# Decode read-out in column groups, output projection taken by token halves, 16 dropped columns, and two state stores ahead of two loads

## The reference, cut to what matters

```python
z, xbc, dt = jnp.split(u @ w_in, ...)
xs, Bm, Cm = jnp.split(silu(conv(xbc)), ...)
y, final = ssd_chunked(xs, dt, A, Bm, Cm, ssm_state, chunk)   # C @ start state, decayed, plus the part within a chunk
y = (y + d_skip * xs) * silu(z)
yg = y.reshape(b, L, SSM_GROUPS, D_INNER // SSM_GROUPS)
y = yg * rsqrt(mean(yg * yg) + EPS) * norm_w
return y @ w_out, new_conv, final
```

## Time and profile before

| | us |
|---|---|
| median of 3 runs | 1124.11 |
| the profiled execution | 1121.49 |
| its span, first to last instruction | 1119.7 |
| PE busy | 1037.6 (93%) |
| DVE busy | 609.9 (54%) |
| ACT busy | 452.2 (40%) |
| POOL busy | 369.3 (33%) |
| mean granted clock of PE | 0.965 |

### The profile page before, as it was taken

How to read it: one execution, slowest core, us unless ns; L and a number is a source line. 1 busy time by engine, 2 the same in 40 slices (tenths; PEclk the granted TensorE clock), 3 DMA queues, 4 the chain that set the end, 5 groups by cost and what they waited for, 6 DMA issues and landing times.

```text
span 1119.7 us, 18856 instructions
## 1 busy us (share of the span) xinstructions
PE 1037.6 (93%) x7568; PEld 962.5 (86%) x7568; DVE 609.9 (54%) x1438; ACT 452.2 (40%) x780; POOL 369.3 (33%) x274
## 2 busy tenths in 40 slices
PE   5999999999999899978888999899989999898978
PEld 4998899889997899768878988898889988898858
DVE  4125421544135322547794679747796567965772
ACT  5334622362334522563224355144542435434252
POOL 1431134213311333116340445315362164540530
PEclk9999999999999999989998899998999999997979
DMA  6422123322223222011325533154331552407202
GB/s 181 154 81 95 39 76 102 111 81 90 79 60 117 89 76 82 20 38 38 98 79 135 151 98 123 40 154 142 88 123 40 153 157 73 150 13 207 76 12 81
DMA packets 144119, 106.37 MB, mean 95 GB/s; under 512 B 10258, under 2 KB 135364, under 8 KB 143840
## 3 DMA queue, kind: packets, MB, share of 16 engines
q1 hardware_dynamic: 117160, 92.10, 26.8%
q10 hardware_dynamic: 26872, 13.06, 4.5%
HBM read 92.42 MB, written 16.79 MB: 98 GB/s over the span
## 4 chain that ended last, share of the span: by engine, by line
PE 65%; DVE 16%; issue 5%; DMA 4%; ACT 3%; POOL 3%; SPq 1%; ACTq 0%; DVEq 0%; POOLq 0%
PE pp L1010 16%; PE pp L1012 15%; PE pp L1011 15%; DVE cv L1658 4%; DVE y_lo L1807 2%; PE pT_ L1248 2%; DMA w_raw_buf<-in_w_attn_out 2%; POOL w_lo_buf L547 2%; PE pS L1106 1%; PE pO L1081 1%; PE pT_ L1298 1%; POOL seg L585 1%; DVE cv L1656 1%; DMA seg<-a_scratch 1%; DVE z L1799 1%
## 5 line engine op out<-in xcount | busy, mean ns | idle before, releaser
L547 POOL TENSOR_TENSOR w_lo_buf<-w_raw_buf,w_hi_buf 128x512 fp32r<-128x512 f32 x226 | 309.6, 1401 | 589.5 <-ACT w_hi_buf L611 453.4
L1010 PE MATMUL pp<-h_hi,w_hi_buf 128*128 128x280 f32 x1280 | 394.7, 308 | 8.4 <-DVE rb L1632 3.2
L1011 PE MATMUL pp<-h_lo,w_hi_buf 128*128 128x280 f32 x1280 | 376.6, 294 | 0.0
L1012 PE MATMUL pp<-h_hi,w_lo_buf 128*128 128x280 f32 x1280 | 376.6, 294 | 0.0
L1010 PEld LDWEIGHTS pp<-h_hi,w_hi_buf 128*128 128x128 f32 x1280 | 245.7, 192 | 20.6 <-issue 12.0
L1011 PEld LDWEIGHTS pp<-h_lo,w_hi_buf 128*128 128x128 f32 x1280 | 245.8, 192 | 4.9 <-issue 4.3
L1012 PEld LDWEIGHTS pp<-h_hi,w_lo_buf 128*128 128x128 f32 x1280 | 245.4, 192 | 0.0
L611 ACT ACTIVATE w_hi_buf<-w_raw_buf 128x2048 fp32r<-128x2048 f32 (+1 forms) x57 | 107.8, 1892 | 31.2 <-PE pp L1012 11.0
L1471 DVE TENSOR_TENSOR x<-x,pp 128x280 f32<-128x280 f32 x128 | 56.3, 444 | 99.6 <-PE pp L1012 99.2
L1010 PE MATMUL pp<-y_hi,w_hi_buf 128*128 128x280 f32 x256 | 80.3, 314 | 13.3 <-DVE y_lo L1807 8.7
L1010 PE MATMUL pp<-og_hi,w_hi_buf 128*128 128x280 f32 x256 | 76.3, 298 | 5.1 <-DVE og_lo L1577 4.6
(11 more groups left out here) (286 smaller groups left out, 1688.5 us busy)
## 6 DMA issues: line engine op xcount, KB each, us to landing
w_raw_buf<-in_w_attn_in SPq DMA_DIRECT2D x16, 1024.0 KB, 5.1
w_raw_buf<-in_w_ssm_in SPq DMA_DIRECT2D x16, 1024.0 KB, 5.5
w_raw_buf<-in_w_attn_out SPq DMA_DIRECT2D x8, 1024.0 KB, 6.5
s_in<-in_state_ssm SPq DMA_DIRECT2D x32, 256.0 KB, 4.2
out<-s_in SPq DMA_DIRECT2D x32, 256.0 KB, 3.5
seg<-a_scratch ACTq DMA_DIRECT2D x16, 512.0 KB, 4.1
w_raw_buf<-in_w_ssm_out SPq DMA_DIRECT2D x8, 1024.0 KB, 5.5
w_raw_buf<-in_w_attn_in SPq DMA_DIRECT2D x8, 512.0 KB, 6.5
```

The lines of the kernel that those rows point to most:

```text
L547: ins = pool.tensor_tensor(w_lo_buf[n % LO_SLOTS][:, piece], raw[n % RAW_SLOTS][:, piece], w_hi_buf[n % HI_SLOTS][:, piece].bitcast(F32), ...
L1010: pe.matmul(dst, hi[:, k, cols], a_hi[:, k, tk], start=(k == 0), stop=False)
L1011: pe.matmul(dst, hi[:, k, cols], a_lo[:, k, tk], start=False, stop=False)
L1012: mm = pe.matmul(dst, lo[:, k, cols], a_hi[:, k, tk], start=False, stop=(k == depth - 1))
```

## The change

- `y_of` is replaced. `y_quad` takes four sequences: for each, 32 columns of weights (`c_own`, the sequence's 4 columns of C among zeros, made by ACT) stand in a column group of their own, and the transposed state streams with 512 columns. Two quads accumulate in one bank. ACT copies the bank out, and `turn_y` multiplies it back into the old layout with four products. There are four `sT` buffers where there were two.
- z and the mixer's output projection leave out the 16 meta columns: halves of 272.
- The output projection goes by blocks of tiles: all first halves, then all second halves (blocks of 4 tiles; in the last stage one block of 8). DVE adds in that order, puts the low parts of y's second part behind the first two adds, and one tap behind each later one.
- DVE's `add_skip(g, 0)` stands behind `prepare(g, 1)` and one evacuation of z.
- SP issues two state stores, then two loads.

```diff
+def out_order(stage):
+    blocks = (range(0, 8),) if stage == STAGES - 1 else (range(0, 4), range(4, 8))
+    return [(t, half) for tiles in blocks for half in range(2) for t in tiles]
+def span(kind, stage, half):
+    if kind == "z" or kind == "out" and stage >= GROUPS:
+        n = SEQ // 2 + SAMPLE // 2
+        return slice(N_META + half * n, N_META + (half + 1) * n)
+    return slice(half * HALF, (half + 1) * HALF)
...
         def part_of(part):
-            return slice(EARLY, T) if part else slice(0, EARLY)
+            return slice(EARLY, T) if part else slice(N_META, EARLY)
...
                     sp.dma_start(rows(ssm_sample, b), s_in[u % STATE_SLOTS][:, :, :]).then_inc(sn_out[u % STATE_SLOTS], 16)
-                    if b + STATE_SLOTS < DEC_B:
-                        load_state(b + STATE_SLOTS)
+                    if b + 1 == DEC_B - STATE_SLOTS:
+                        for later in range(STATE_SLOTS, DEC_B):
+                            load_state(later)
...
+                if i == 1:
+                    act.wait_ge(c_zero, 1)
+                    act.wait_ge(act_ready, k + 1)
+                    step, last_b = SAMPLE + DEC_S, (DEC_B - 1) * DEC_S
+                    act.activation(c_own[:, 0:(DEC_B - 1) * step].rearrange("p (b s) -> p b s", s=step)[:, :, 0:DEC_S],
+                                   bc[:, 1, PROMPT:PROMPT + last_b].rearrange("p (b s) -> p b s", s=DEC_S), ACT.Copy)
+                    act.activation(c_own[:, (DEC_B - 1) * step:], bc[:, 1, PROMPT + last_b:T],
+                                   ACT.Copy).then_inc(c_own_ready, 1)
...
-                    act.activation(sT[b % 2][:, :], pO[:, b % 2, :], ACT.Copy).then_inc(sT_ready, 1)
+                    act.activation(sT[b % 4][:, :], pO[:, b % 2, :], ACT.Copy).then_inc(sT_ready, 1)
                 split_hi()
+                act.wait_ge(yo_done, 3 * g + 2)
+                act.activation(sT[1][:, :], pT_[:, 1, :], ACT.Copy).then_inc(yo_copied, 1)
...
-                def y_of(b):
-                    pe.wait_ge(sT_ready, DEC_B * g + b + 1)
-                    c0 = PROMPT + b * DEC_S
-                    for t in range(HEADS):
-                        mm = pe.matmul(pT_[:, 1, t * SAMPLE + b * DEC_S:t * SAMPLE + (b + 1) * DEC_S],
-                                       sT[b % 2][:, t * P:(t + 1) * P], bc[:, 1, c0:c0 + DEC_S], start=True, stop=True)
+                def y_quad(i):
+                    pe.wait_ge(c_own_ready, g + 1)
+                    for j in range(4):
+                        b = 4 * i + j
+                        pe.wait_ge(sT_ready, DEC_B * g + b + 1)
+                        mm = pe.matmul(pT_[SAMPLE * j:SAMPLE * (j + 1), 1, :], c_own[:, b * SAMPLE:(b + 1) * SAMPLE],
+                                       sT[j][:, :], start=(i == 0), stop=(i == 1))
                     mm.then_inc(yo_done, 1)
...
-                    y_of(2 * pair)
-                    y_of(2 * pair + 1)
+                    if pair % 2:
+                        y_quad(pair // 2)
+            def turn_y(g):
+                pe.wait_ge(yo_copied, g + 1)
+                for t in range(HEADS):
+                    mm = pe.matmul(pT_[:, 1, t * SAMPLE:(t + 1) * SAMPLE], sT[1][:, t * P:(t + 1) * P],
+                                   cst[:, C_SUM4:C_SUM4 + SAMPLE], start=True, stop=True)
...
-                    for t in range(8):
-                        tile_of("out", s - 1, t)
+                    for t, half in out_order(s - 1):
+                        project("out", s - 1, t, half)
...
                 project("z", s, *part.pop(0))
+                turn_y(g)
...
-                    low_y(g - 1, 1)
...
-                    for t in range(8):
-                        add_out(s - 1, t)
-                        for n in (2 * t, 2 * t + 1):
-                            if n < 12:
-                                conv_tap(g, 3 + n // 4, n % 4)
+                    for n, (t, half) in enumerate(out_order(s - 1)):
+                        add_out(s - 1, t, (half,))
+                        if n < 2:
+                            low_y(g - 1, 1, (2 * n, 2 * n + 1))
+                        elif n < 14:
+                            conv_tap(g, 3 + (n - 2) // 4, (n - 2) % 4)
...
-                add_skip(g, 0)
                 prepare(g, 1)
                 evac_z()
+                add_skip(g, 0)
```

More of the change, by code:

```diff
@@ L90, in shape_constants, with add @@
     return c
+def out_order(stage):
[6 more added lines that the diff above has]
+    return slice(half * HALF, (half + 1) * HALF)
 def plan():
     slabs, halves = [], []
-    def add(kind, stage, count, tiles_per_slab, first=0):
-        for i in range(first, first + count):
+    def add(kind, stage, count, tiles_per_slab):
+        for i in range(count):
             slabs.append((kind, stage, i))
+            if kind == "out" and stage >= GROUPS:
+                continue
             for t in range(tiles_per_slab * i, tiles_per_slab * (i + 1)):
@@ L102, in add @@
                     halves.append((kind, stage, t, half))
+        if kind == "out" and stage >= GROUPS:
+            halves.extend((kind, stage, t, half) for t, half in out_order(stage))
     for s in range(GROUPS):
@@ L534, in _ @@
             pool.memset(eps[:, 1:2], EPS * P).then_inc(ones_ready, 1)
+            pool.memset(c_own[:, :], 0.0).then_inc(c_zero, 1)
             done = [0]
@@ L993, in project @@
                 cols = slice((tile % per) * P, (tile % per + 1) * P)
-                tk = slice(half * HALF, (half + 1) * HALF)
+                tk = span(kind, s, half)
                 if kind == "out":
@@ L1429, in result @@
                 pe.transpose(dst[0:32, 512:640], x[:, t, PROMPT:T], ident).then_inc(yt_done, 1)
-            for t in range(8):
-                tile_of("out", STAGES - 1, t)
-                if t:
+            for n, (t, half) in enumerate(out_order(STAGES - 1)):
+                project("out", STAGES - 1, t, half)
+                if n == 0:
+                    final_state(GROUPS - 1)
+                if half and t:
                     result(t - 1)
-                else:
-                    final_state(GROUPS - 1)
             result(7)
@@ L1456, in bank @@
             def bank(kind, s, tile, half):
-                j = half_no[(kind, s, tile, half)]
+                j, tk = half_no[(kind, s, tile, half)], span(kind, s, half)
                 dve.wait_ge(p_done, j + 1)
-                return pp[:, j % 2, 0:HALF]
+                return pp[:, j % 2, 0:tk.stop - tk.start]
             def scaled(dst, kind, s, tile, parts=(0, 1)):
@@ L1466, in scaled, with add_out @@
                                       ALU.mult).then_inc(p_evac, 1)
-            def add_out(s, tile):
-                for half in range(2):
-                    tk = slice(half * HALF, (half + 1) * HALF)
+            def add_out(s, tile, halves=(0, 1)):
+                for half in halves:
+                    tk = span("out", s, half)
                     dve.tensor_tensor(x[:, tile, tk], x[:, tile, tk], bank("out", s, tile, half),
@@ L1800, in norm_y, with low_y @@
                                              ALU.mult, ALU.mult).then_inc(yn_ready, 1)
-            def low_y(g, part):
+            def low_y(g, part, tiles=range(HEADS)):
                 tk, done = part_of(part), 8 * g + 4 * part
-                for t in range(HEADS):
+                for t in tiles:
                     dve.wait_ge(og_hi, 4 * GROUPS + done + t + 1)
@@ L1938, in _ @@
                 low_y(GROUPS - 1, part)
-            for t in range(8):
-                add_out(STAGES - 1, t)
+            for t, half in out_order(STAGES - 1):
+                add_out(STAGES - 1, t, (half,))
 _INS = ["x_prompt", "x_sample", "cache_k", "cache_v", "state_conv", "state_ssm", "meta_tokens", "norm_w",
```

28 lines of the change are left out of this document (17 added, 11 removed).

## The result

| | before | after |
|---|---|---|
| median (range, runs) | 1124.27 us (1123.35 to 1124.81, 4) | 1084.67 us (1084.22 to 1087.12, 4) |
| profiled execution, span | 1121.49, 1119.7 | 1085.0, 1083.2 |
| mean granted clock | 0.965 | 0.98 |

The ratio of the times is 0.9656, 95% interval 0.964 to 0.9671: about 38.7 us less, where 42.5 were forecast for the profiled execution, which lost 36.5.

The account below looks back on a forecast made before the run. PE was taken as the bound (busy 93%, 65% of the chain of waits). Terms of 17.2 + 3.2 + 10.5 + 6.6 + 5.0 = 42.5 us off a 1124.1 us median gave 1082 us, range 1068 to 1102.

Parts of the forecast that it names:

- Term 1: Output projections of stages 1 to 3: the new order shortens each window to 26.0 us, 17.2 us less in all.
- term 3: State read-out, groups 0 to 2: two quads and `turn_y` replace four blocks, 10.5 us less.
- term 4: Behind the read-out, groups 0 to 2: two thirds of the half-clock loss of 9.9 us goes, 6.6 us less.
- term 5: Group 3: last state load issued some 2.5 us earlier, four read-out blocks replaced by quads; 5.0 us less.
- Waits for `x` adds and none for low parts: Sign in the output projections, expected with windows at about 26 us: PE waits for DVE's additions only.
- Term 2: z and the last output projection: eight columns fewer save 3.3 ns a matmul, 3.2 us less.
- No wait for a state load in group 3: Sign in group 3: PE, which stood 1.43 us for the last sequence's load, no longer waits.
- Clock as before: Rival: the clock falls as before, since transposes and small products stay; 1088 us, chance 0.15.
- DVE takes the gain: Rival at the output stage: DVE's slots stand in PE's way, windows of 29 us; 1091 us, chance 0.14.
- No overlap of four: Rival in the read-out: column groups run one after another, 3.4 us a quad, 20 more; 1102 us, chance 0.12.
- Slower: Rival in the read-out: quads run one after another and at half clock; 1133 us, chance 0.03.

Follow-up runs that it names:

- e2: Kernel after, with the mixer's output projection tile by tile again and DVE's low parts ahead of the additions: 1100.02 us.
- e7: Kernel after, keeping PE's new output order, but DVE makes all low parts of y's second part before the additions: 1095.47 us.
- e1: Kernel after, with z and the output projection in halves of 280 columns again: 1089.37 us.
- e3: Kernel after, with the old read-out of the states (`y_of` and its additions) put back: 1099.62 us.
- e4: Kernel after, with all eight read-out products of a group one after another in one column group: 1094.91 us.
- e8: Kernel after, POOL's subtraction and ACT's clamp for one head of eight, exponent scaled, part of the computation left out: 1069.61 us.
- e6: Kernel after, with ACT issuing the next segment load ahead of this segment's decays: 1083.44 us.
- e9: Kernel after, with the four `ec` loads issued behind the read-out's copy and not between two state copies: 1090.49 us.
- e11: Kernel after, with POOL's subtraction for the full segments moved to ACT as a bias, one activation per head, nothing left out: 1083.17 us.

## Why the prediction was right, point by point

The time of 1084.67 us lies 2.7 us above the forecast of 1082. For the profiled execution, from which the terms were read, it was 1079, and that one took 1085.0: 6 us off. Term 1 held in mechanism and size. Of the others the mechanisms held in the main but not the sizes: term 3 brought far less than was put down, term 4 more, and term 5 came out for another reason than the one given. That the sum came out as near as it did is in part luck.

**Term 1, the output projection: right.** 25.93 us a window for a forecast of 26.0, so 17.5 us for 17.2. Undoing the order (e2) costs 13.3 in the whole. What the prediction named as late next, DVE, is what remains: PE is idle 0.4 us of 25.5. "Waits for `x` adds and none for low parts" was half right: 1.3 us for additions, and 1.5 for low parts, 0.9 of them in the third window. That the interleaving matters as much as the order (e7) is what the step-by-step play of DVE's queue had assumed.

**Term 2, columns: somewhat too large.** A matmul is 2.4 ns shorter and not 3.3, so 960 of them give 2.3 us for 3.2; e1, with 1536, gives 2.2 to 4.7 us. The columns of the output windows, put in term 1, bring nothing there.

**Term 3, the read-out: right where it stands, too large in the sum.** The quad was put at 0.96 us and takes 1.00; the second one 1.31 for 1.26; `turn_y` 0.80 for 0.95. Four column groups run side by side. In the Trainium skill ("TensorE: Matmul & The Clock Gate", Part 3) three column tiles give 2.38 times and four row tiles 3.07. Here four column tiles of 32 columns take 1.06 us against 3.62 in one group: 3.4 times. The step that failed is the missing one. Nothing was said of the rounds behind the read-out, where the segment's chain of 8.0 us a round came out as the bound once PE arrived early. e3, e4 and e8 show it: 22 us of terms 3 to 5 undone cost 12.4, 20 us of serial passes cost 8.2, and the chain cut short gives 15.0. By the stages, groups 0 to 2 lost 14.9 us outside the output windows. Their three half-clock stretches are some 10.2 of that by estimate, and the columns 1.4, so about 3 us are left of the 10.5 of this term.

**Term 4, the clock: right and rather more.** Two thirds of 9.9 us were taken; the stretches are gone in all three groups, 20.4 us at half clock and so some 10.2 us for 6.6. They are gone from the three boundaries as well, where the stall for low parts had been. e3 brings back those behind the read-out, e7 those at the boundaries (6.8, 3.4 and 3.4 us). e2 has the waits for low parts again and only one of the three (3.4 us at 831.8), so what made them is not shown. The rule weighed against it, that transposes don't keep the clock (the Trainium skill, same page, Part 4), did not make the drops stay. The transposes are as they were, and quads of 512 columns stand in place of the long blocks of 4. No run takes the transposes away, and none sets the blocks' going apart from the quads' coming.

**Term 5, group 3: wrong in its cause.** "No wait for a state load in group 3" failed. Both loads are issued right behind the two stores, in one piece:

```profile
983.74 0.94 SPq L528 DMA_DIRECT2D out<-s_in  x2
986.11 1.34 SPq L503 DMA_DIRECT2D s_in<-in_state_ssm  x2
```

PE can start on the first only at 991.5, 5.4 us after its issue. The DMA engines are busy 97% of the time from 986 to 993; the transfers of `seg` and `ec` (five by ACT from 985.69 to 988.8) are under way at the same time. PE has run ahead meanwhile, so it waits longer than before:

```profile
991.54 0.66 PE L1303 MATMUL pO<-cst,s_in 128*128 128x128 f32 x4 [2.61 <-DMA s_in<-in_state_ssm]
993.37 1.12 PE L1303 MATMUL pO<-cst,s_in 128*128 128x128 f32 x4 [1.17 <-DMA s_in<-in_state_ssm]
```

Behind it the clock falls for 10.2 us, for 13.7 in the earlier trace rows. From the output projection at the head of its stage to the end the kernel is 11.7 us shorter (138.0 for 149.7), of which 5.0 are the window's and 6.7 are left, for 5.0 of this term and 1.3 of term 2. The load didn't bring them. By estimate most came with the clock, which the term priced only at the read-out: 27.3 us of this stretch were at half clock before (13.7, 3.4 and 10.2), and 17.1 are now (10.2 and 6.8), some 5.1 us.

**The sum.** By stages (start of one output projection to the next): 12.5, 10.2 and, to the end, 11.7 us less; 4.7 less in group 0's stage before the first. The part ahead of it, which the change doesn't touch, took 2.6 us more in this one execution; one half-clock stretch more there (3.4 us at 371.5) is at most 1.7 of them. Of the 36.5 us, 17.5 are the windows. The other 19.0, or 21.6 without that part, stand against a forecast of 25.3 for terms 2 to 5. The missing 4 us are what is left of two larger errors, term 3 some 7 us too large and term 4 some 4 too small. The view of waits puts the new waits before `part_b` at 3.6 us (11.2 for 7.6), and e8 shows that it doesn't hold all that the loop costs.

**The rivals.** Clock as before: excluded by the windows. DVE takes the gain: excluded (25.9, not 29). No overlap of four: excluded by the starts; its price, checked in e4, was 8 to 10 and not 20. Slower: with it.

## What to carry to other kernels

A shorter block on the bounding engine is worth its length only until the next chain of other engines catches up. Before forecasting, take the period of each loop that runs beside the engine (here load, POOL, ACT, DVE over two buffers: 8.0 us a round against 6.8) and cap the gain of the rounds behind it. Changing the order on one engine needs its partner's queue changed with it: e7 has PE's new order alone, and is nearly as slow as the old one. The granted clock belongs in the sum for each stage: here it gave about half of the gain, where the forecast had put down 6.6 us. And an in-order queue that issues transfers as well as arithmetic turns each wait of a transfer into a stall of the arithmetic behind it (e6, e9, e11).

## What the runs showed of the hardware

- Four fp32 products with 32 weight columns each, in four column groups, 512 columns streamed: starts 7 ns apart, two rounds of passes 0.43 us apart, all in 1.06 us; one after another in the same group 3.62 us.
- A projection's matmul starts every 0.1261 us with 272 columns and 0.1284 with 280, at granted clock 1.00: 2.4 ns for 8 columns.
- An operation of DVE can last as long as POOL's one beside it. An addition of 128x128 behind `turn_y` runs from 751.21 to 753.17, POOL's subtraction of a segment from 751.13 to 753.02; in e11, where POOL is idle there, the addition takes 0.29 us. The one of 128x512 at 766.22 takes 2.14 us beside such a subtraction, and 0.69 in e11.
- Eight activations of 128 columns follow at 0.29 us each (2.45 us in all), one of 1024 takes 1.06.
